# Last sums of a forward transform tree: from VectorE to accumulating matmuls, with scaling on ScalarE

## The reference, cut to what matters

```
filt_f = jnp.fft.rfft(hyena_filters(L, lp), n=2 * L, axis=0)
resp = filt_f[:, 0] + jnp.conj(filt_f[:, 1])
z = v
for o, gate in enumerate((x1, x2)):
    zf = jnp.fft.rfft(z, n=2 * L, axis=1)
    conv = jnp.fft.irfft(zf * resp[None, :, o], n=2 * L, axis=1)[:, :L]
    z = gate * (conv + z * bias[o])
return z.astype(h.dtype) @ lp['w_out']
```

## Time and profile before

| | |
|---|---|
| median of 3 runs | 4398.41 us (4397.34 to 4398.62) |
| the profiled execution's own time | 4397.87 us |
| its span | 4396.1 us |
| PE / PEld busy | 4010.8 / 3370.8 us (91% / 77%) |
| DVE busy | 2366.4 us (54%) |
| ACT busy | 1085.8 us (25%) |
| POOL busy | 1150.3 us (26%) |

### The profile page before, as it was taken

The page is one execution under the profiler, slowest core; times in us unless marked ns, Lnnn a source line. Parts: engine busy times, 40 slices in busy tenths (PEclk is TensorE's granted clock), DMA queues, the critical chain, the costliest instruction groups (busy, mean ns, idle before and its releaser), DMA issues.

```text
span 4396.1 us, 51614 instructions
## 1 busy us (share of the span) xinstructions
PE 4010.8 (91%) x22024; PEld 3370.8 (77%) x22024; DVE 2366.4 (54%) x2626; ACT 1085.8 (25%) x1568; POOL 1150.3 (26%) x587
## 2 busy tenths in 40 slices
PE   5999899989899999999699999976659899999998
PEld 3787788887688888888477777765548788888887
DVE  4382555542545434445576755699961544555444
ACT  4253333331311111111333234111111311111112
POOL 2111544433422222222410000122213322222224
PEclk7999999999899999999799999888879899999999
DMA  7511000011121222221222222321320111111111
GB/s 256 173 32 38 25 1 1 20 39 53 53 63 53 64 65 58 60 63 49 89 71 86 78 85 95 126 110 62 119 75 23 36 35 38 39 39 35 40 38 70
DMA packets 309676, 280.95 MB, mean 64 GB/s; under 512 B 9013, under 2 KB 285958, under 8 KB 305959
## 3 DMA queue, kind: packets, MB, share of 16 engines
q1 hardware_dynamic: 309448, 277.65, 19.3%
HBM read 219.94 MB, written 57.67 MB: 63 GB/s over the span
## 4 chain that ended last, share of the span: by engine, by line
PE 68%; DVE 15%; issue 2%; DMA 2%; ACT 2%; POOL 2%; SPq 0%; POOLq 0%; DVEq 0%; ACTq 0%
PE PS L670 49%; DVE piece L1811 8%; PE PS L1879 5%; PE PS L1187 3%; PE PS L1182 2%; PE PS L2052 1%; DVE piece L1219 1%; PE PS L1184 1%; DMA piece<-hyena_tokens 1%; PE PS L1652 1%; DVE piece L2220 1%; DVE piece L2506 1%; DVE piece L2248 0%; ACT piece L510 0%; POOL piece L2626 0%
## 5 line engine op out<-in xcount | busy, mean ns | idle before, releaser
L670 PE MATMUL PS<-piece,piece 128*128 128x512 f32 (+1 forms) x13896 | 2798.0, 361 | 58.3 <-POOL piece L545 31.4
L670 PEld LDWEIGHTS PS<-piece,piece 128*128 128x128 f32 x13896 | 2312.8, 190 | 522.9 <-issue 99.1
L653 POOL TENSOR_TENSOR piece<-piece,piece 128x1024 fp32r<-128x1024 f32 (+2 forms) x213 | 507.2, 2382 | 2535.7 <-ACT piece L647 2535.7
L1879 PE MATMUL PS<-piece,piece 128*128 128x256 f32 x1920 | 439.2, 391 | 127.2 <-DVE piece L2506 111.9
L1747 DVE SCALAR_TENSOR_TENSOR piece<-piece,piece,piece 128x1024 f32<-128x1024 f32 x352 | 532.6, 1513 | 12.6
L1879 PEld LDWEIGHTS PS<-piece,piece 128*128 128x128 f32 x1920 | 374.8, 197 | 186.7 <-DVE piece L2506 114.7
L1767 DVE SCALAR_TENSOR_TENSOR piece<-PS,piece,piece 128x1024 f32<-128x1024 f32 (+1 forms) x256 | 214.6, 880 | 373.8 <-PE PS L670 373.8
L647 ACT ACTIVATE piece<-piece 128x1024 fp32r<-128x1024 f32 (+2 forms) x213 | 208.1, 977 | 666.4 <-PE PS L670 618.0
L1744 DVE TENSOR_SCALAR piece<-piece,piece 128x1024 f32<-128x1024 f32 x44 | 35.8, 813 | 514.7 <-ACT piece L1694 514.7
L1219 DVE TENSOR_TENSOR piece<-piece,PS 128x512 f32<-128x512 f32 x188 | 127.2, 685 | 207.0 <-PE PS L1187 169.6
L1697 ACT ACTIVATE piece<-piece 128x1280 f32<-128x1280 f32 x44 | 56.1, 1275 | 606.2 <-DVE piece L1755 606.2
(11 more groups left out here) (242 smaller groups left out, 3479.2 us busy)
## 6 DMA issues: line engine op xcount, KB each, us to landing
piece<-in_l_ffn_up SPq DMA_DIRECT2D x88, 512.0 KB, 3.8
piece<-in_l_w_in SPq DMA_DIRECT2D x45, 512.0 KB, 3.8
piece<-in_l_ada_w SPq DMA_DIRECT2D x44, 512.0 KB, 5.2
piece<-in_l_ada_w SPq DMA_DIRECT2D x18, 1024.0 KB, 7.0
piece<-in_l_ffn_down SPq DMA_DIRECT2D x48, 384.0 KB, 3.0
piece<-filters_s SPq DMA_DIRECT2D x8, 2176.0 KB, 9.4
filters_s<-piece SPq DMA_DIRECT2D x64, 256.0 KB, 2.0
hyena_tokens<-piece SPq DMA_DIRECT2D x24, 640.0 KB, 4.0
```

Source lines behind the costliest of these rows:

```text
L653: eng.tensor_tensor(LO[i % 2][0][:, 0:n], RAW[i % raws][:, 0:n], HI[i % 2][1][:, 0:n], ALU.subtract)\
L670: m = eng.matmul(PS[:, bank + b, 0:n], w, x[:, a:a + n], start=first and n_ == 0, stop=last and n_ == 2)
L1879: m = eng.matmul(PS[:, bank, o * HC:(o + 1) * HC], M[i][o], rhs[i], start=i == 0, stop=i == 1)
```

## The change

A second tree, `fold_tree`, is added beside `tree`, and the main loop uses it; the filters keep `tree`. It leaves out the last `plus` and `minus` of three butterflies, and so has 14 instructions in place of 20. `T` gets the turned pair alone. For leaves 2 to 7 `transform` now gets two pairs of operands, x0 (from K) and the turned pair (from T), and accumulates over both: eight matmuls in place of four. The turned pair has to be scaled by plus or minus the sine: the new function `scaled` on ScalarE makes for each of the three butterflies a copy times minus the sine for the odd leaf (`n`), then scales the pair in place for the even leaf (`w`).

In ScalarE's program `scaled` of job k + 1 stands behind the copies of job k and ahead of `spread`; `scaled` of job 0 stands ahead of the loop. In `first_leaves` leaf 2 is left out, and is made with the rest of job 0. The waits of SyncE on the tree's last step name its new last step.

```diff
+        N_FOLD = 14
+        PAIRS = ((2, math.pi / 4, 5), (4, math.pi / 8, 11), (6, 5 * math.pi / 8, 13))
+        def fold_tree(eng, st, tag, rnd, Z, K, T):
+            run = chain(eng, st, tag, rnd)
+            def turned(x1r, x1i, m, th, out, at):
+                ratio = math.cos(th) / math.sin(th)
+                run(eng.scalar_tensor_tensor, row(out, at, m), x1r, ratio, x1i, ALU.mult, ALU.subtract)
+                run(eng.scalar_tensor_tensor, row(out, at + m, m), x1i, ratio, x1r, ALU.mult, ALU.add)
+            run(eng.tensor_tensor, row(K, 0, 4), row(Z, 0, 4), row(Z, 4, 4), ALU.add)
+            run(eng.tensor_tensor, row(K, 4, 4), row(Z, 0, 4), row(Z, 4, 4), ALU.subtract)
+            run(eng.tensor_tensor, row(T, 0, 2), row(K, 0, 2), row(K, 2, 2), ALU.add)
+            run(eng.tensor_tensor, row(T, 2, 2), row(K, 0, 2), row(K, 2, 2), ALU.subtract)
+            turned(row(K, 5, 1), row(K, 7, 1), 1, math.pi / 4, T, 4)
+            turned(row(Z, 2, 2), row(Z, 6, 2), 2, math.pi / 4, K, 0)
+            x1 = row(K, 0, 4).rearrange("p (u c) -> p u c", u=2)
+            for at, sign in ((8, 1), (12, -1)):
+                run(eng.scalar_tensor_tensor, row(K, at, 4).rearrange("p (u c) -> p u c", u=2), x1, sign * math.sin(math.pi / 4), pair(Z, 0, 4, 2), ALU.mult, ALU.add)
+            turned(row(K, 9, 1), row(K, 11, 1), 1, math.pi / 8, T, 8)
+            turned(row(K, 13, 1), row(K, 15, 1), 1, 5 * math.pi / 8, T, 12)
...
-        def transform(eng, bank, M, rhs):
+        def transform(eng, bank, M, *rhs):
             for o in range(2):
                 for i in range(2):
-                    m = eng.matmul(PS[:, bank, o * HC:(o + 1) * HC], M[i][o], rhs[i], start=i == 0, stop=i == 1)
+                    for n_, r_ in enumerate(rhs):
+                        m = eng.matmul(PS[:, bank, o * HC:(o + 1) * HC], M[i][o], r_[i], start=i == 0 and n_ == 0, stop=i == 1 and n_ == len(rhs) - 1)
...
                 eng.wait_ge(acT.sem, acT.at("e", n_t - 2))
-                for l in range(3):
+                for l in range(2):
                     leaf_forward(eng, "s", l, 0)
...
                 if g == "s":
-                    eng.wait_ge(veT.sem, veT.at(leaf_step[l], k))
-                    rhs = [TB2[k % 2]["s"][:, 2 * l + u, :] for u in range(2)]
+                    K, T = KB2[k % 2]["s"], TB2[k % 2]["s"]
+                    rhs = [[T[:, 2 * l + u, :] for u in range(2)]]
+                    if l < 2:
+                        eng.wait_ge(veT.sem, veT.at(f"zt{2 + l}", k))
+                    else:
+                        eng.wait_ge(acZ.sem, acZ.at(f"{'wn'[l % 2]}{l}", k))
+                        x0 = 2 * (l - l % 2)
+                        rhs = [[K[:, x0 + 2 * u, :] for u in range(2)]] + rhs
...
+            def scaled(eng, k):
+                T = TB2[k % 2]["s"]
+                for l, th, made in PAIRS:
+                    eng.wait_ge(veT.sem, veT.at(f"zt{made}", k))
+                    eng.activation(row(T, 2 * l + 2, 2), row(T, 2 * l, 2), ACT.Copy, scale=-math.sin(th)).then_inc(*acZ.did(f"n{l + 1}", k))
+                    eng.wait_ge(acZ.sem, acZ.at(f"n{l + 1}", k))
+                    eng.activation(row(T, 2 * l, 2), row(T, 2 * l, 2), ACT.Copy, scale=math.sin(th)).then_inc(*acZ.did(f"w{l}", k))
...
-                tree(eng, veT, "zt", k, Z[k % 2], 0, Z[k % 2], 0, KB2[k % 2]["s"], TB2[k % 2]["s"])
+                fold_tree(eng, veT, "zt", k, Z[k % 2], KB2[k % 2]["s"], TB2[k % 2]["s"])
...
-                        rest = range(3, 8)
+                        rest = range(2, 8)
...
+                scaled(eng, 0)
                 for k, (c, order) in enumerate(QUEUE):
                     for g in "ps":
                         for l in LEAVES[g]:
                             eng.wait_ge(peI[g].sem, peI[g].at(f"i{l}", k))
                             eng.activation(row(TB2[k % 2][g], 2 * l, 2), PS[:, bank_of(g, "i", l), :], ACT.Copy).then_inc(*acC[g].did(f"i{l}", k))
+                    if k + 1 < nj:
+                        scaled(eng, k + 1)
                     if k - 1 in turns and k < nj - 1:
                         spread(k - 1)
```

More of the change, by code:

```diff
@@ L2287, in mixer_hyena @@
             peZ, peI, acC, veC, veU, smC = {}, {}, {}, {}, {}, {}
-            veT = steps("ve_conv_tree", [f"zt{i}" for i in range(N_TREE)], nj)
+            veT = steps("ve_conv_tree", [f"zt{i}" for i in range(N_FOLD)], nj)
+            acZ = steps("ac_conv_turned", sum([[f"n{l + 1}", f"w{l}"] for l, _, _ in PAIRS], []), nj)
             for g in "sp":
@@ L2297, in mixer_hyena @@
             peO, acO, veO = steps("pe_turn", ["t0", "t1"], NCH), steps("ac_turn", ["hi0", "hi1"], NCH), steps("ve_turn", ["lo0", "lo1"], NCH)
-            leaf_step = {l: f"zt{i}" for l, i in enumerate((2, 3, 6, 7, 14, 15, 18, 19))}
             def last_leaf(g):
@@ L2356, in leaf_forward @@
                 if g == "s":
-                    eng.wait_ge(veT.sem, veT.at(leaf_step[l], k))
-                    rhs = [TB2[k % 2]["s"][:, 2 * l + u, :] for u in range(2)]
-                else:
-                    rhs = [Z[k % 2][:, NS // P + u, :] for u in range(2)]
-                transform(eng, bank_of(g, "z", l), matrices(FW, l, False), rhs).then_inc(*peZ[g].did(f"z{l}", k))
+                    K, T = KB2[k % 2]["s"], TB2[k % 2]["s"]
[6 more added lines that the diff above has]
+                        rhs = [[K[:, x0 + 2 * u, :] for u in range(2)]] + rhs
+                else:
+                    rhs = [[Z[k % 2][:, NS // P + u, :] for u in range(2)]]
+                transform(eng, bank_of(g, "z", l), matrices(FW, l, False), *rhs).then_inc(*peZ[g].did(f"z{l}", k))
+            def scaled(eng, k):
[5 more added lines that the diff above has]
+                    eng.activation(row(T, 2 * l, 2), row(T, 2 * l, 2), ACT.Copy, scale=math.sin(th)).then_inc(*acZ.did(f"w{l}", k))
             def start_tree(eng, k):
@@ L2390, in _ @@
                     if order and c + 2 < NCH:
-                        eng.wait_ge(veT.sem, veT.at(f"zt{N_TREE - 1}", k))
+                        eng.wait_ge(veT.sem, veT.at(f"zt{N_FOLD - 1}", k))
                         eng.wait_ge(peZ["p"].sem, peZ["p"].at("z1", k))
@@ L2538, in _ @@
                 spread(nj - 1)
-            done = [peO, acO, veO, veT] + [x[g] for x in (peZ, peI, acC, veC, smC, veU) for g in "sp"]
+            done = [peO, acO, veO, veT, acZ] + [x[g] for x in (peZ, peI, acC, veC, smC, veU) for g in "sp"]
             x_ready, part3 = project(A["l1_w_out"], done, done, 1, (s_x, 32))
```

## The result

The changed kernel takes 4414.79 us (median of 5 runs, 4413.99 to 4418.64), the kernel before, beside it on the same chip, 4398.02 us (5 runs, 4395.28 to 4398.62). The ratio is 1.0042, with a 95% interval of 1.0027 to 1.0057: slower by 0.4%. The forecast was 4416 us.

The account below looks back on a forecast made before the run. VectorE was taken to bound the ordinary jobs, busy 50.2 to 50.6 of 52.15 us. Job 0 (5.0), ordinary jobs (1.3), jobs 3 and 4 (8.2) and job 7 (3.45) summed to 18.0 us more: 4416 us, range 4404 to 4427.

Parts of the forecast that it names:

- 2.78 us of slack on TensorE: Job 1: ScalarE's last copy ends 2.78 us before VectorE reaches untree, which needs it.
- The tree saves 4.3 us: VectorE, each job: six instructions of 128x512 leave the tree, 0.72 us each, 4.3 us together.
- 3.45 us behind the restart: TensorE: added matmuls of leaves 6 and 7, after its restart at leaf 6, delay all ten inverse transforms by 3.45 us.
- the four ordinary jobs: Jobs 1, 2, 5 and 6: the last copy becomes later than VectorE, making intervals longer, together 1.3 us.
- The clock does not stay up in a gap of 5.3 us: TensorE's wait before its restart shrinks from 15 to about 5.3 us; the low clock stretch was assumed to remain.
- Jobs 3 and 4: Gate of p and untree come 4.1 us late through later leaves and scalings ahead of spread; 8.2 us for both.
- Job 0: Nothing hides its scalings, and leaves of eight matmuls delay the last copy: untree 5.0 us later.
- Job 7: No tree to run, and untree already waited for the last copy: 3.45 us later in full.
- Two signs: Expected in the trace: job 7's wait for the last copy about 15 us; ordinary intervals 52.1 to 52.9 us.
- The first rival (the clock stays up): TensorE's clock stays up in ordinary jobs and job 7 as the gap shrinks: +6.5 us, 4405 us; chance 8%.
- the second (dear scalings): ScalarE's scalings cost 1.05 us each, so jobs 3 and 4 cost 13.2 us, job 0 another 0.8: 4422 us; chance 7%.
- The third rival (faster): Added matmuls of leaves 6 and 7 cost less than the slack, so VectorE's saving decides: 4383 us; chance 9%.

Follow-up runs that it names:

- e7: Kernel before the change, with leaf 5 of s made eight times more ahead of TensorE's restart from job 1 on: 4391.19 us, ratio 0.9989 to the kernel before.
- e5: Changed kernel without the 24 matmuls a job over x0, so the transform is not computed: 4379.74 us, ratio 0.9964 to the kernel before.
- e2: Changed kernel with the full tree in job 0 and leaves 0 and 1 of s moved last: 4388.57 us, ratio 0.9979 to the kernel before.
- e3: Changed kernel with the change for leaves 2 to 5 only; leaves 6 and 7 keep last sums on VectorE: 4388.70 us, ratio 0.9980 to the kernel before.
- e6: Changed kernel with scaled placed behind spread in ScalarE's program: 4409.69 us in its one execution.
- e1: Changed kernel, but job 0 alone uses the full tree and four matmuls for each leaf: 4406.04 us, ratio 1.0024 to the kernel before.
- e8: Changed kernel with full tree in job 0, leaves 0 and 1 last, scaled behind spread, restart gap partly filled with repeated matmuls: 4371.84 us, ratio 0.9946 to kernel before.
- e4: Changed kernel, but from job 1 on TensorE makes leaf 5 of s twice ahead of its restart: 4406.98 us, ratio 1.0026 to the kernel before.

## Why the prediction was right

- **VectorE bound the ordinary jobs, with 2.78 us of slack on TensorE.** Shown by e7 (more work and full clock on TensorE, same 52.2 us) and e5 (VectorE's saving alone: 49 us, where the loop through TensorE had been put at 49.4).
- **The tree saves 4.3 us.** VectorE's busy time fell from 50.2 (job 1) to 45.9.
- **3.45 us behind the restart turn the bound over.** The wait for leaf 7 (2.99 us) and for the last copy (1.74 us) appeared where they were placed. e2 shows that it is the place and not the amount, e3 that without leaves 6 and 7 there is a gain. For the four ordinary jobs 1.3 us were forecast and 2.8 measured. The difference is the clock: in jobs 2 and 6 TensorE was 47.9 and 48.2 us busy, in job 1 46.6. The low stretch behind R was 1.3 and 1.6 us dearer in those than in job 1.
- **The clock does not stay up in a gap of 5.3 us.** The gap was 5.38 us and a low stretch followed each; in job 1 the clock was 0.56 for 3.35 us:

```profile
2903.55:2906.90 3.35, 3.35 (x9) 2.76 (x10) 3.35 (x5) 0.00 (x0) 3.35 (x4) 0.56 0.76 309
```

- **Jobs 3 and 4: 4.1 us forecast, 4.0 and 3.6 measured, in job 3 with two terms off that cancel.** The last copy in job 3 ended at R + 26.8, 3.8 later than before and not 3.45 (the clock again). The scalings took 3.56 us (3035.49 to 3039.05), not 3.85, and e6 shows that they cost 0.1 us and not 0.65, since the load of X is ready at nearly the same time.
- **Job 0: 5.0 forecast, 5.0 measured.** From the first leaf to `untree` it is 51.5 us in place of 46.5, and e1 shows that nothing makes up for it. That undoing it gives 7.5 was not in the working: there was a gain of 2.4 to be had, from job 1's short tree.
- **Job 7: 3.45 forecast, 2.5 measured.** TensorE's busy time rose from 23.78 to 26.30 us there: the added 3.45, less 0.9 for a shorter low stretch.
- **Two signs did not show as written.** Job 7's wait for the last copy stayed at 11.69 us and did not grow to 15: everything that VectorE does after leaf 7 moved with it, and the 2.5 us are in the wait for leaf 7. And the ordinary intervals went up to 53.56, past the 52.9 named, by the clock.

The sum came out at 17.9 us against 18.0, and that close a hit is luck: ordinary jobs were 1.5 us dearer than forecast, jobs 3 and 4 0.6 and job 7 0.9 cheaper, and these cancel. The mechanism is what was right.

The first rival (the clock stays up) fell by the low stretch behind every gap of 5.38 us, the second (dear scalings) by their 0.61 to 0.63 us each. The third rival (faster) fell by the size of two leaves: 3.45 us against a slack of 2.78. e5, which takes the added matmuls away, came out at 15.7 us under the kernel before; the rival had 15.

The advice of the Trainium skill, "Perfetto Trace Analysis", section "Optimizing Scalar/DVE Operations", that with VectorE saturated some work may be moved to ScalarE, was no wrong one here: the scalings ahead of spread cost 0.1 us in jobs 3 and 4 (e6), and in job 0 they cost about 1.3, where TensorE waits for two of them. What cost the rest was the part of the work that went to TensorE, behind the point at which VectorE releases it.

## What to carry to other kernels

Before work is moved off the engine that bounds a loop, measure how far behind it the next cycle runs (here 2.78 us), and place the moved work in that engine's queue ahead of the point where it waits, not behind: with job 0 kept as it was, the change with its 24 added matmuls a job cost 9.6 us in one order (e1) and gained 7.9 in the other (e2). A job at the edge of the pipeline, where nothing hides the added steps, deserves its own form.

## What the runs showed of the hardware that I had not expected

TensorE's clock is worth a place in such a sum even for gaps of 2 us. The runs with restarts behind gaps of different lengths give this tally, one execution each. Full clock means that TensorE's busy time was the lowest seen for its number of records, as 20.99 us for 96 or 41.71 for 192:

| gap ahead of R, us | runs | full clock behind it |
|---|---|---|
| 0.66 to 1.69 | e7 (two), e8 (seven) | 9 of 9 |
| 1.92 to 2.03 | e4 (five), e7 (one) | 4 of 6 |
| 2.99 | e2 (five) | 2 of 5 |
| 3.56 to 4.03 | e7 (four) | 0 of 4 |
| 5.38 | after the change, e1, e6 (five each), e3 (three) | 0 of 18 |

A gap of one length was followed by either level, so its length alone does not decide; what else does is open. Filling the gaps with repeated matmuls, which compute nothing new, went with full clock behind every restart of e8. Held against the one profile of e2, the clock is most of what jobs 1 to 7 have over it: 1.4 and 1.7 us in jobs 5 and 6, 1.7 in each of 3 and 4, 2.9 in 7, out of 10.3.
